# The first loads of a decoder layer cut and reordered, and TensorE's first transposes and multiplications put in the same order

## The reference

```python
h = rms_norm(x, norm1_w)                 # x: (256, 1024)
proj = h @ w_in                          # w_in: (1024, 3072)
rq, rk, rv, rg, mq, mk, mv = split(proj)
ret  = silu(rg) * group_norm(retention(rotary(rq), rotary(rk), rv))
moba = causal_attention(rotary(mq), rotary(mk), mv)      # 256 tokens: one block
x = x + concat(ret, moba) @ w_out
h2 = rms_norm(x, norm2_w)
# 32 experts, top 4 of each token; w1: (32, 1024, 2048), w2: (32, 1024, 1024)
x = x + sum_over_top4(gate * (clamped_swiglu(h2 @ w1[e] + b1[e]) @ w2[e] + b2[e]))
out = rms_norm(x, final_norm_w)
```

## Time and profile before

| | us |
|---|---|
| median of 3 runs | 1052.78 |
| lowest, highest | 1052.59, 1054.54 |
| the profiled execution's own time | 1053.78 |
| its span, first to last instruction | 1052.0 |

### The profile page before, as it was taken

How to read it: one execution, slowest core, us unless ns; L and a number is a source line. 1 busy time by engine, 2 the same in 40 slices (tenths; PEclk the granted TensorE clock), 3 DMA queues, 4 the chain that set the end, 5 groups by cost and what they waited for, 6 DMA issues and landing times.

```text
span 1052.0 us, 11246 instructions
## 1 busy us (share of the span) xinstructions
PE 1028.2 (98%) x4918; PEld 415.7 (40%) x4918; DVE 221.5 (21%) x585; ACT 117.5 (11%) x223; POOL 0.2 (0%) x4
## 2 busy tenths in 40 slices
PE   9999999999999999999999999999999999998996
PEld 8888543333333333333333333333333333323332
DVE  2173442111111111111111111111111111111111
ACT  2131130000000000000000000000000000000002
POOL 0000000000000000000000000000000000000000
PEclk9999999999999999999999999999999999999999
DMA  9982999999999999999999999999999999999995
GB/s 320 369 363 80 351 371 386 410 429 434 420 424 400 437 427 430 434 428 429 427 425 431 434 429 430 430 430 433 424 427 428 433 432 427 433 428 426 428 422 224
DMA packets 39126, 424.62 MB, mean 404 GB/s; under 512 B 3512, under 2 KB 16320, under 8 KB 19744
## 3 DMA queue, kind: packets, MB, share of 16 engines
q1 hardware_dynamic: 38768, 423.51, 96.3%
q10 hardware_dynamic: 304, 0.33, 0.1%
HBM read 422.78 MB, written 1.05 MB: 403 GB/s over the span
## 4 chain that ended last, share of the span: by engine, by line
PE 92%; DMA 5%; another core or an unknown queue 1%; DVE 1%; issue 0%; ACT 0%; SPq 0%; DVEq 0%; ACTq 0%
PE PS L1444 41%; PE PS L1466 20%; PE PS L1122 8%; PE PS L1415 5%; DMA ring<-in_w 5%; PE PS L1398 5%; PE PS L1303 3%; PE PS L1259 3%; PE PS L1497 2%; PE PS L1407 2%; PE PS L1390 1%; DMA ring<-in_w_in 1%; PE PS L1571 0%; PE PS L1585 0%; PE PS L1192 0%
## 5 line engine op out<-in xcount | busy, mean ns | idle before, releaser
L1444 PE MATMUL PS<-ring,work 128*64 128x512 f32 x2040 | 448.7, 596 | 12.0 <-DMA ring<-in_w 10.7
L1444 PEld LDWEIGHTS PS<-ring,work 128*64 128x64 f32 x2040 | 143.9, 137 | 291.9 <-issue 273.4
L1466 PE MATMUL PS<-ring,work 128*64 128x512 f32 x1024 | 227.4, 595 | 0.1
L1466 PEld LDWEIGHTS PS<-ring,work 128*64 128x64 f32 x1024 | 70.6, 137 | 153.8 <-issue 151.1
L1015 DVE TENSOR_SCALAR work<-PS 128x512 f32<-128x512 f32 x32 | 22.1, 692 | 401.1 <-PE PS L1444 401.1
L1122 PE MATMUL PS<-ring 128*128 128x256 f32 x384 | 85.4, 380 | 0.3 <-DMA ring<-in_w_in 0.3
L644 ACT ACTIVATE work<-work 128x512 f32<-128x512 f32 x32 | 20.2, 630 | 535.3 <-DVE work L1015 535.3
L1122 PEld LDWEIGHTS PS<-ring 128*128 128x128 f32 x384 | 72.0, 190 | 10.8 <-DMA ring<-in_w_in 0.7
L983 DVE TENSOR_TENSOR work<-PS,n2w 128x512 f32<-128x512 f32 x30 | 20.8, 692 | 228.3 <-PE PS L1407 228.3
L1415 PE MATMUL PS<-late,work 64*128 64x512 f32 x248 | 61.9, 616 | 0.0
L1398 PE MATMUL PS<-resid,work 128*64 128x512 f32 x248 | 58.5, 592 | 0.0
(11 more groups left out here) (173 smaller groups left out, 370.2 us busy)
## 6 DMA issues: line engine op xcount, KB each, us to landing
ring<-in_w SPq DMA_DIRECT2D x48, 4096.0 KB, 34.9
ring<-in_w SPq DMA_DIRECT2D x85, 2048.0 KB, 27.1
ring<-in_w SPq DMA_DIRECT2D x18, 1024.0 KB, 9.7
ring<-in_w_in SPq DMA_DIRECT2D x11, 1024.0 KB, 11.9
ring<-in_w_out SPq DMA_DIRECT2D x4, 1024.0 KB, 12.1
ring<-in_w SPq DMA_DIRECT2D x6, 512.0 KB, 6.9
ring<-in_w_in SPq DMA_DIRECT2D x2, 512.0 KB, 6.3
ring<-in_consts SPq DMA_DIRECT2D x1, 800.0 KB, 11.2
```

The lines of the kernel that those rows point to most:

```text
L1444: last = mm(bank(v)[64 * half:64 * half + 64, :], gh[:, c, :], w[:, v * F + half * BANK:v * F + (half + 1) * BANK], start=False, stop=(c = ...
L1466: last = mm(out[64 * half:64 * half + 64, :], aT_n[:, c, 64 * h:64 * h + 64], ring[:, 2 * d + c // 2, cols:cols + BANK], start=(h == 0 and ...
```

## The change

The 512 KB of tile 1 of x are now loaded as two halves, like those of tile 0, each with a semaphore of its own. The order of the first loads was: x tile 0 first half, x tile 0 second half, weight chunk 0 first half, x tile 1, weight chunk 0 second half. It becomes: x tile 0 first half, weight chunk 0 first half, x tile 0 second half, weight chunk 0 second half, x tile 1 first half, x tile 1 second half. The loads after these keep their order. TensorE's transpositions of the second half of tile 0, and of both halves of tile 1, are put between the multiplications of weight chunk 0, and tile 1's multiplications are split by a wait for `hT_ready` 3 and one for 4.

```diff
-        x_in = [sem(f"x_in{k}") for k in range(T + 1)]
+        x_in = [sem(f"x_in{k}") for k in range(2 * T)]
...
-            for half in range(2):
-                sp.dma_start(resid[:, 0, half_cols(half)], x_v[:, 0, half_cols(half)]).then_inc(x_in[half], 16)
+            def load_x(t, half):
+                sp.dma_start(resid[:, t, half_cols(half)], x_v[:, t, half_cols(half)]).then_inc(x_in[2 * t + half], 16)
+
+            load_x(0, 0)
             load_win(0, 0, C // 2, win0_in)
-            sp.dma_start(resid[:, 1, :], x_v[:, 1, :]).then_inc(x_in[2], 16)
+            load_x(0, 1)
             load_win(0, C // 2, C, head_full[0])
+            load_x(1, 0)
+            load_x(1, 1)
             load_win(1, 0, C, head_full[1])
...
             for t in range(T):
-                if t == 0:
-                    act.wait_ge(x_in[0], 16)
-                act.wait_ge(x_in[t + 1], 16)
+                act.wait_ge(x_in[2 * t], 16)
+                act.wait_ge(x_in[2 * t + 1], 16)
...
             def transpose_x(t, half):
-                pe.wait_ge(x_in[half if t == 0 else 2], 16)
+                pe.wait_ge(x_in[2 * t + half], 16)
...
             transpose_x(0, 0)
             pe.wait_ge(n1w_in, 16)
             nc.tensor.transpose(bank(6)[:, 0:C], n1_rows, ident[0:C, 0:C]).then_inc(n1wT_done, 1)
-            transpose_x(0, 1)
             keep_warm(WARM_WIN)
...
                 pe.wait_ge(win0_in, 16)
                 pe.wait_ge(hT_ready, 1)
-                project_part(0, 0, 0, C // 2)
-                for half in range(2):
-                    transpose_x(1, half)
+                project_part(0, 0, 0, 2)
+                transpose_x(0, 1)
+                project_part(0, 0, 2, 4)
                 pe.wait_ge(head_full[0], 16)
                 pe.wait_ge(hT_ready, 2)
-                project_part(0, 0, C // 2, C)
+                project_part(0, 0, 4, 6)
+                transpose_x(1, 0)
+                project_part(0, 0, 6, 8)
+                transpose_x(1, 1)
+                pe.wait_ge(hT_ready, 3)
+                project_part(0, 1, 0, 4)
                 pe.wait_ge(hT_ready, 4)
-                project_part(0, 1, 0, C).then_inc(chunk_used, 1)
+                project_part(0, 1, 4, 8).then_inc(chunk_used, 1)
```

## The result

The changed kernel is slower, by about a quarter of a percent: a median of 1057.24 us over 20 executions (1054.69 to 1062.56) beside 1054.31 us for the kernel before over 20 of its own (1052.36 to 1059.8). The ratio is 1.0026, with a 95% interval of [1.0014, 1.0039]. Forecast were 1052.3 us and a gain of 0.5; the range ended at 1054.4. The median of three executions that I started from, 1052.78, lay 1.5 us under the one over 20, which explains part of the distance; the 2.9 us between the two kernels are another matter.

The account below looks back on a forecast made before the run. TensorE bounds the head; the weight stream it starts sets the end. First counting wait 3.64 us earlier, less 1.73 for passes, 1.32 for transpositions and 0.1 for waiting: 0.5 gained, 1052.3 us against the median; range 1050.9 to 1054.4.

Parts of the forecast that it names:

- What bounds the kernel: Whole kernel: the weight stream sets the end, and a shift of chunk 0's end moves the kernel's end equally.
- The landings by bytes: First loads: bytes issued ahead set landings; weight halves at 5.9 and 8.59 us, x tiles complete at 6.93 and 10.04.
- The step that failed: First multiplication of chunk 0: its input hT 1 is there at 6.37 us unchanged, so it starts at 6.45, not 6.94.
- The starting loss: Weight chunk 0's multiplications: 0.25 us lost in starting, added once, moving the chunk's end from 14.77 to 15.0 us.
- the 0.1 us that the sum had for waiting: After eight passes of chunk 0: TensorE waits for the weights' second half (8.59) and hT 2 (8.65), losing about 0.1 us.
- The clock: Head, rival at 0.05: TensorE may pause before 6.45, the clock stays at 1.2 GHz, 8.2 us more, ending at 1060.5.
- The sum: End of weight chunk 0: 15.0 instead of 15.53 us, 0.5 gained; bounds 0.8 gained to 0.9 lost.

Follow-up runs that it names:

- short kernels: Kernels cut off behind weight chunk 1: before 28.00 and 27.87 us, changed 29.43 and 29.56, changed with 34 instead of 26 first dummy multiplications 28.30 (medians).
- a_again: The changed kernel run once more, against the kernel before: median 1057.06 us over 12 executions, ratio 1.0013 [0.9993, 1.0033].
- ident_warm: Whole changed kernel with the identity issued first on SyncE's queue and 30 and 17 dummy multiplications: median 1053.38 us, ratio to before 0.9988 [0.9967, 1.0009].
- after_look: One more execution of the whole changed kernel, nothing altered, for another trace: 1056.74 us.
- after: The changed kernel against the kernel before, in its first profiled execution: 1055.43 us.
- pe_only: TensorE's new order with the old loads, against the kernel before: median 1057.05 us over 12 executions, ratio 1.0016 [1.0, 1.0032].
- loads_only: The new loads with TensorE's old order, against the kernel before: median 1057.12 us over 13 executions, ratio 1.0016 [1.0003, 1.003].

## Why the prediction was wrong

**What bounds the kernel:** right, as far as traces show it. By the end of the 64 passes at 281 the profiled execution was 1.7 us behind that of before (296.87 against 295.17), and 1.5 of them were still there at the first wait for weights, 815.22 against 813.70. For the head's own loss it is argued from the medians: 1.4 to 1.7 us in the short kernels, 1.4 (`a_again`) and 2.7 by the two ratios of the whole ones.

**The landings by bytes:** right to 0.3 us on SyncE's queue in the profiled execution (x tile 0 at 7.2 for 6.93, tile 1 at 9.9 for 10.04, the halves of weight chunk 0 at 6.2 for 5.9 and 8.5 for 8.59). They vary, though: in the profiled execution of `ident_warm` x tile 0's second half landed only at 8.3, TensorE waited 0.83 us for it, and chunk 1 ended at 23.1.

**The step that failed:** "hT 1 is there at 6.37, and nothing in the change moves it (it hangs on the identity, ...)". The identity is on another queue, yet with weights next in line on SyncE's instead of x it took 4.1 us from issue to landing instead of 3.3. That the two loads share the DMA engines is the likely reason; the runs show only that the order on one queue moved the landing on the other. hT 1 was there at 6.75 and the first product at 6.89 instead of 6.45, 0.44 us late, and it would have been later had the clock not been up at 4.92. The larger price of the late identity is the gap of 0.9 to 1.1 us that it opens in TensorE's work, and with it the clock (below): 1.3 us between the short kernels with and without that gap (29.56 and 28.30), which the sum put at nothing.

**The starting loss:** counted once, as 0.25 us; TensorE paid it twice. Four passes took 1.10 us at 6.89 and again at 9.30, and 0.87 at 8.42 and 10.84. The rest of the 0.6 us by which the forecast was off is this second loss, less the 0.1 us that the sum had for waiting, so that at full clock the whole forecast gain is used up: chunk 0 ended at 12.14 + 16 x 0.216 = 15.60, forecast 15.0, before 15.53.

**The clock:** the rival was named, with the wrong place, a chance of 0.05, and "the pause is at most 0.4 us". The late identity made it 0.9 to 1.1 us, and ahead of 4.9, not of 6.45. Also the price was taken as all or nothing (8.2 us), where the rows show a rise some us late or one fall of 3.4 us: 1.2 us in `after_look`, 1.4 to 1.7 in the short kernels' medians. Before the change the same slow passes cost nothing, since TensorE waited for 10.09 anyway. The sentence of the Trainium skill that I weighed (TensorE: Matmul & The Clock Gate, The HAM clock gate), that the moment differs from run to run, was the one to act on. The traces bear it out: the same first four transpositions of the changed kernel took 1.11 us in one and 0.66 in another.

**The sum:** 0.5 us gain forecast; measured in the head from 0.0 (`after`, `a_again`, full clock) to 1.7 us of loss (short kernels' medians), mostly the latter. That is shown. The remainder of the 2.9 us, 1.2 to 1.5, is not settled. It can hardly be told from nothing, since the interval of the loss, [1.5, 4.1] us (1.0014 to 1.0039), begins where the head's loss ends.

Two things in the later kernel could fill it. The falls near 145 us cost about 5 us each; executions with a mean clock of 0.992 or less, to which such a fall belongs, were 9 of the 33 with the change and 10 of the 68 before it for which this number is on record. Without them the medians are 1056.4 and 1054.5 us, 1.9 apart. And smaller falls, like that at 281 us with its 1.6 to 3.3 us in the seven traces, seem more frequent: a mean clock of 0.996 or more was found in 6 of the 33 and in 30 of the 68, though a fall in the head lowers it too. Whether a head that ends 1.5 us later meets such falls more often, or this is chance, no run tells.

## What to carry to other kernels

A transfer on another queue is not free of a reordering: look up each thing that the first instruction of the critical chain waits for, and which loads are under way beside it. Work moved out of a waiting time takes its cover along: where dummy or early work kept TensorE's clock up until real work arrived, a gap of 1 us in it can cost 1.5 us afterwards, and only many executions show it, not one trace: of the two first traces of the changed kernel neither had lost anything in the head. When a change acts in the first 2% of a kernel, cut the kernel off there and time that: a loss of 1.5 us was clear in six executions of 28 us and unclear in twelve of 1055.

## What the hardware did that I had not expected

- The clock falls with TensorE busy all the time: near 281 us, during or behind eight passes with a stationary operand of 32 rows (1.54 us lost over 64 passes in the profiled execution after the change, 2.64 in `pe_only`). So it was in seven of the eight traces of whole kernels; in the one of before the same passes stood at the same place, and it did not fall.
- In the short kernel it fell again at 7 us after having risen, behind 1.04 and 0.37 us of idleness; in the whole kernel before, waits for weights of 1.61 and 1.62 us at 813.70 and 842.91 left it at 1.00.
- At the router's stage of short, scattered passes it fell in two of the eight traces, `a_again` and `loads_only`, and stayed down for some 10 us (0.63, 0.50, 0.59 in three stretches of 4 us of `a_again`); the DMA share went down to 0.28 with it.
